# Gated linear attention groups: outputs ahead of the sample states' products, their sums behind the next weight's split

## The reference, cut to what matters

```python
o = einsum('bhts,bhsv->bhtv', att, vc) + einsum('bhtk,bhkv->bhtv', qc * exp(b), S)
S = exp(b_last)[..., 0, :, None] * S + einsum('bhsk,bhsv->bhkv', kc * exp(b_last - b), vc)
...
oa = merge(rmsnorm(oa, gn_a)) * silu(ga)      # and the same for GLA: ob
x = x + concatenate([oa, ob]) @ w_out
```

## Time and profile before

| what | us |
|---|---|
| median of 3 runs | 2837.17 |
| the profiled execution, its own time | 2839.51 |
| its span (first to last instruction) | 2837.9 |
| PE busy, share of the span | 2686.3, 95% |
| VectorE busy | 1864.8, 66% |
| ScalarE busy | 1282.3, 45% |
| GpSimd busy | 1343.1, 47% |

### The profile page before, as it was taken

How to read it: one execution, slowest core, us unless ns; L and a number is a source line. 1 busy time by engine, 2 the same in 40 slices (tenths; PEclk the granted TensorE clock), 3 DMA queues, 4 the chain that set the end, 5 groups by cost and what they waited for, 6 DMA issues and landing times.

```text
span 2837.9 us, 52238 instructions
## 1 busy us (share of the span) xinstructions
PE 2686.3 (95%) x19130; PEld 2546.6 (90%) x19130; DVE 1864.8 (66%) x2876; ACT 1282.3 (45%) x2311; POOL 1343.1 (47%) x1458
## 2 busy tenths in 40 slices
PE   7899999999989999998899999999998999999996
PEld 7899999888888999998899998787887789899996
DVE  7878866754547887758877864352635257877765
ACT  5565554222135566545565652222222225565552
POOL 3577743432225778613677753120303014777731
PEclk9999999999989999999999999999999999999998
DMA  3233322121112323232233223332333322223321
GB/s 128 72 95 98 92 93 77 62 74 54 46 60 69 96 88 97 86 105 68 67 104 94 87 99 141 112 119 87 118 113 121 104 85 76 86 87 105 92 95 54
DMA packets 109044, 255.71 MB, mean 90 GB/s; under 512 B 12496, under 2 KB 37216, under 8 KB 108800
## 3 DMA queue, kind: packets, MB, share of 16 engines
q1 hardware_dynamic: 96192, 206.73, 22.7%
q0 software_dynamic: 12608, 45.75, 4.4%
HBM read 227.65 MB, written 24.77 MB: 89 GB/s over the span
## 4 chain that ended last, share of the span: by engine, by line
PE 57%; DVE 7%; issue 3%; ACT 3%; POOL 1%; DVEq 0%; ACTq 0%; POOLq 0%
PE ps L981 27%; PE ps L568 12%; PE ps L590 11%; PE ps L837 1%; PE ps L901 1%; ACT wh L1108 1%; DVE ff_hidden_sums L1965 1%; PE ps L845 1%; ACT ps L1277 1%; DVE wl L1617 1%; PE ps L822 1%; DVE ff_x_low L1841 1%; DVE ff_blocks_b L1936 1%; DVE wl L1862 1%; PE ps L911 1%
## 5 line engine op out<-in xcount | busy, mean ns | idle before, releaser
L1862 DVE TENSOR_TENSOR wl<-ps,wh 128x512 fp32r<-128x512 f32 (+1 forms) x480 | 303.5, 632 | 150.7 <-ACT ps L1277 82.8
L1617 DVE TENSOR_TENSOR wl<-raw,wh 128x1024 fp32r<-128x1024 f32 x169 | 226.5, 1340 | 201.3 <-ACT wh L1108 200.6
L1108 ACT ACTIVATE wh<-raw 128x1024 fp32r<-128x1024 f32 x169 | 178.4, 1056 | 399.0 <-PE ps L568 200.8
L981 PE MATMUL ps<-ff_x_high,wh 128*128 128x288 f32 x1152 | 342.0, 297 | 12.6 <-DVE ff_c L1890 12.6
L981 PE MATMUL ps<-ff_x_low,wh 128*128 128x288 f32 x1152 | 341.3, 296 | 0.0
L981 PE MATMUL ps<-ff_x_high,wl 128*128 128x288 f32 x1152 | 340.4, 296 | 0.0
L590 PE MATMUL ps<-xh,wh 128*128 128x288 f32 x1248 | 299.4, 322 | 19.0 <-DVE xl L1639 15.2
L1277 ACT ACTIVATE ps<-ff_w_sums 128x512 f32<-128x512 f32 (+1 forms) x352 | 190.7, 551 | 269.0 <-POOL ff_w_sums L2550 261.6
L981 PE MATMUL ps<-ff_x_high,ff_more_high 128*128 128x288 f32 x864 | 256.2, 297 | 24.6 <-DVE ff_hidden L1899 10.3
L590 PE MATMUL ps<-xh,wl 128*128 128x288 f32 x1248 | 272.3, 300 | 0.0
L590 PE MATMUL ps<-xl,wh 128*128 128x288 f32 x1248 | 270.4, 299 | 0.0
(11 more groups left out here) (343 smaller groups left out, 7374.3 us busy)
## 6 DMA issues: line engine op xcount, KB each, us to landing
raw<-in_w SPq DMA_DIRECT2D x169, 512.0 KB, 3.5
raw<-in_w SPq DMA_DIRECT2D x288, 256.0 KB, 2.6
raw<-in_w SPq DMA_DIRECT2D x192, 192.0 KB, 2.3
rS<-in_s_ret POOLq DMA_DIRECT2D x28, 512.0 KB, 6.9
out_ret_s<-rS POOLq DMA_DIRECT2D x28, 512.0 KB, 3.7
x<-in_xT SPq DMA_DIRECT2D x8, 288.0 KB, 6.6
out_yT<-x SPq DMA_DIRECT2D x8, 288.0 KB, 2.2
S<-in_s_hgrn POOLq DMA_DIRECT2D x4, 512.0 KB, 3.6
```

The source lines that it names most:

```text
L981: last = nc.tensor.matmul(bank(w, q), lhsT=slot(w, q, wt)[:, t], rhs=rhs, start=(k == 0 and (wt, r) == (0, 0) and q in (1, 5, 2)), stop=(k ...
L1108: nc.scalar.activation(wh[:, n.mod(2), :], raw[:, r, :], ACT.Copy).then_inc(S("hi_made"), 1)
L1617: nc.vector.tensor_tensor(wl[:, n.mod(2), :], raw[:, n.mod(NRAW), :], wh[:, n.mod(2), :], ALU.subtract)\
L1862: nc.vector.tensor_tensor(slot(w, q, 1)[:, c], src[:, c], slot(w, q, 0)[:, c], ALU.subtract)\
```

## The change

In PE's table `state_sample` and `outputs(0)` change places. For HGRN it is now outputs behind quarter 1 of unit 3 and sample products behind quarter 2. For GLA the outputs of head 0 stand alone behind quarter 1 of unit 5, and the sample products behind the outputs of head 1. `outputs(0)` now waits itself for the last picks and for St, as `state_sample` did. VectorE's work on the sample states is in two functions: the decay product stays where it was, now followed by `keys_ready`; the sum goes behind the split. In the last group both go behind the second head's `heads_output`, and GpSimd does `heads_low` before the store of Sn and waits for the stores afterwards.

```diff
                     pe.wait_ge(S("S0_in"), count("S0_in", G("S0_in", 16)))
+                    pe.wait_ge(S("picked"), count("picked", G("picked", 8 * ns)))
+                    pe.wait_ge(S("turned_out"), count("turned_out", G("turned_out", 2 * ns + 3)))
...
-                    (3, 0): [state_prompt], (3, 1): [state_sample], (3, 2): [lambda: outputs(0)],
+                    (3, 0): [state_prompt], (3, 1): [lambda: outputs(0)], (3, 2): [state_sample],
...
-                    (5, 0): [state_prompt], (5, 1): [state_sample, lambda: outputs(0)],
-                    (5, 2): [lambda: head_norm(ns, i, pair, 0)], (5, 3): [lambda: outputs(1)],
+                    (5, 0): [state_prompt], (5, 1): [lambda: outputs(0)],
+                    (5, 2): [lambda: head_norm(ns, i, pair, 0)], (5, 3): [lambda: outputs(1), state_sample],
...
-            dve.wait_ge(S("S0_in"), count("S0_in", G("S0_in", 16)))
-            Tb = U[:, TP:T].rearrange("p (b t) -> p b t", t=LS)[:, :, LS - 1:LS].broadcast_to([P, NBAT, P])
-            nc.vector.tensor_tensor(Sn[:, :, :], S0[:, :, :], Tb, ALU.mult).then_inc(S("s_new"), 1)
-            dve.wait_ge(S("s_new"), count("s_new", G("s_new", 1)))
-            dve.wait_ge(S("turned"), count("turned", G("turned", k + 1)))
-            nc.vector.tensor_tensor(Sn[:, :, :].rearrange("p (a b) k -> p a (b k)", a=2),
-                                    Sn[:, :, :].rearrange("p (a b) k -> p a (b k)", a=2), ps[:, 6:8, :], ALU.add)\
-                .then_inc(S("turned_out"), 1)
+            if not following:
+                return
+            sample_decayed(ns, i, pair)
             if following == "hgrn":
                 keys_ready(i, 1)
+            split(n + (2 * ns + 3))
+            sample_added(ns, i, pair)
             if following:
-                split(n + (2 * ns + 3))
...
                     heads_output(2, None, 1, 1, heads=[r])
+                sample_decayed(2, None, 1)
+                sample_added(2, None, 1)
...
+            if pair == 1:
+                heads_low(2, None, 1, 1)
             reached = early(pool, count("turned_out", G("turned_out", 2 * ns + 4)))
...
-            pool.wait_ge(S("S_out"), count("S_out", G("S_out", 32 * (s + 1) // ns)))
+            if pair != 1:
+                pool.wait_ge(S("S_out"), count("S_out", G("S_out", 32 * (s + 1) // ns)))
...
-                heads_low(2, None, 1, 1)
+                pool.wait_ge(S("S_out"), count("S_out", group_count("S_out", 2, None, 1, 32)))
```

More of the change, by code:

```diff
@@ L1810, in gated_group, with sample_decayed, sample_added @@
                         .then_inc(S(f"taken{(u + (2 * ns + 1)).mod(2)}"), 1)
+        def sample_decayed(ns, i, pair):
+            G = lambda name, k: group_count(name, ns, i, pair, k)
+            U = gU[:, :] if ns == 1 else decay[:, pair, :]
+            k = 2 * ns + 3
+            dve.wait_ge(S("S0_in"), count("S0_in", G("S0_in", 16)))
+            Tb = U[:, TP:T].rearrange("p (b t) -> p b t", t=LS)[:, :, LS - 1:LS].broadcast_to([P, NBAT, P])
+            nc.vector.tensor_tensor(Sn[:, :, :], S0[:, :, :], Tb, ALU.mult).then_inc(S("s_new"), 1)
+            dve.wait_ge(S("s_new"), count("s_new", G("s_new", 1)))
+        def sample_added(ns, i, pair):
+            G = lambda name, k: group_count(name, ns, i, pair, k)
+            dve.wait_ge(S("turned"), count("turned", G("turned", 2 * ns + 4)))
+            nc.vector.tensor_tensor(Sn[:, :, :].rearrange("p (a b) k -> p a (b k)", a=2),
+                                    Sn[:, :, :].rearrange("p (a b) k -> p a (b k)", a=2), ps[:, 6:8, :], ALU.add)\
+                .then_inc(S("turned_out"), 1)
         def ffn(norm, n, u, j0, units):
```

## The result

The changed kernel takes **2850.53 us** (median of 5 executions, 2840.91 to 2856.5) against 2837.09 for the kernel before beside it (5 executions, 2834.51 to 2839.3): a ratio of 1.0039, interval 1.0025 to 1.0053. That is slower, above the forecast of 2840.8 and above the range's upper end of 2846.5.

| execution, us | mean granted clock |
|---|---|
| 2840.91 | 0.981 |
| 2840.95 (the profiled one, span 2839.3) | 0.981 |
| 2850.53 | 0.978 |
| 2852.41 | 0.976 |
| 2856.5 | 0.974 |

A forecast was written before the change was run, and what follows sets the result against it. TensorE, busy 95% of the span, was taken to bound the kernel, so only its waits count. Terms 3.23 + 0.9 - 0.5 = +3.6 us gave 2840.8 us; range 2834.5 to 2846.5.

The forecast's parts named there:

- Step 1: HGRN group ends: outputs ahead of sample products only pass on the wait for St; gain 0.
- Step 2: Three HGRN-to-HGRN starts: the sum behind the split delays scaled queries, sigmoid, root and scores; +3.23 us, bounds 0 and 3.9.
- Step 3: First GLA start: GpSimd's store of Sn waits for the sum, delaying loads and second scores; +0.9 us, bounds 0 and 1.5.
- The 0 in the HGRN groups: HGRN starts, GpSimd's queue: the sum ends within 0.3 us of when PE wants it; cost 0, bound 0.3 each.
- Step 4: Last group: moved products gain 0.9 us, the decay product delaying the low part costs 0.4; together -0.5, bounds -3.2 and +1.6.
- Rival (a): Group starts or outputs behind the St wait: idle PE brings more clock dips, 1.7 us each; 2844 to 2846 us, chance 0.22.

The follow-up runs named there:

- e5: The kernel before with only TensorE's new order in the four HGRN groups and the two new waits in `outputs`: 2839.92 us, ratio 1.0016.
- e10: The changed kernel with VectorE's sum moved behind the scaled queries at the three HGRN starts: 2845.89 us, ratio 1.0041.
- e12: e10 with S0's load waiting for the decay product and the store of Sn behind level 2 of the next group: 2843.1 us, ratio 1.0014.
- e4: The kernel before with only the last group's part of the change: 2838.21 us, ratio 1.0002.
- e3: The changed kernel with the last group's old order back on TensorE, VectorE and GpSimd: 2848.76 us, ratio 1.0041.
- e0: The changed kernel again with no edit, 12 executions: 2844.56 us, ratio 1.0030 to the kernel before.
- e8: The kernel before with only VectorE's sum moved behind the split, at the five places with a following group: 2847.31 us, ratio 1.0042.
- e1: The changed kernel with the sum moved back ahead of the split: 2842.64 us, ratio 1.0019.
- e13: The changed kernel with the HGRN sample products moved from behind quarter 2 to behind quarter 3: 2836.74 us, ratio 0.9999.
- e7: e4 with the last group's sample products moved behind the second head's head sums and block 6: 2834.82 us, ratio 0.9995.

## Why the prediction was wrong

**Step 1, outputs ahead, 0: wrong, and the main reason why the result left the range.** The reasoning on waits held; the wait for St passed to L724 (0.25 us), and ScalarE still waited for the unit. It missed what TensorE's clock does when the products, four matmuls in 3.78 us at half clock, follow a quarter behind the outputs: a dip of 5.1 us in place of 1.7. In the HGRN groups alone (e5) it cost +3.4 ± 1.7 us of clock and +1.2 ± 0.6 besides, which is not explained; at the end of the first GLA group it cost 1.7 more in every trace.

**Step 2, the sum in the chain, +3.23: right in mechanism, near in size.** The root's wait went from 0.28 to 1.37, 1.40 and 1.39; the first two stretches grew by 1.36 and 1.25, for 1.14 each. The third start was set at 0.95 from a stretch with a dip in it, which had hidden part of the chain; at full clock it waits as the others do.

**Step 3, GpSimd's queue: right in mechanism, the wait too small.** The wait before the second scores of the first GLA group was forecast at 0.9 (bounds 0 and 1.5) and came as 1.60. How much of it lasts isn't shown: the stretches around it grew by 0.59 and 0.18 only, the second with the gain of the earlier outputs in it. The 0 in the HGRN groups held for the changed kernel, whose trace has no wait of L633 there, and by the reason given: "PE, itself late by then". But that is true only as long as the root is later, and it hides a second chain of nearly the same length. e10 took the first away and the second came up at about the same price; e12 took both, and the cost was gone. As the two run side by side their prices don't add.

**Step 4, the last group, -0.5 (bounds -3.2 and +1.6): inside.** e4 measured -1.0 ± 0.7 and e3 against e0 -1.4 ± 0.8 at full clock (the profiled execution shows -0.22). The half clock moved as step 4 feared, from the outputs to the products. The sign by which it was to be known failed: the wait for the low part should have shrunk and grew, 5.58 to 6.30. From the head sums to the low part's start it was 9.30 us before (789.48 to 798.78) and after (791.01 to 800.31), but TensorE, with less of that stretch at half clock, reached its wait 4.75 us behind the head sums for 5.26, and the low part then took longer. VectorE's timeline and GpSimd's after the change:

```profile
799.43 1.22 DVE L1817 TENSOR_TENSOR Sn<-S,decay 128x1024 f32<-128x1024 f32 x1
```

```profile
800.31 1.60 POOL L2516 TENSOR_TENSOR hid_low<-sqsum,hid_high 128x576 fp32r<-128x576 f32 x1 [8.91 <-ACT hid_high L1436]
```

The low part began 0.08 us behind ScalarE's high part (L1436, to 800.23), as before the change, and so was not held back in its start; but it ran beside the last 0.34 us of the decay product and took 1.60 us for 1.40 in the earlier trace rows. So the decay product cost 0.20 and not 0.4. It is 1.60 or 1.61 in all twelve traces in which the decay product lies there and 1.40 in the four in which it doesn't (before, e3, e5, e8). The Trainium skill, page "SBUF — State Buffer", section "SBUF: two separate sides", has the one that comes second wait for the other's whole instruction. The trace agrees in direction: the low part ended 1.26 us behind the decay product, near its 1.40 alone. But no run put another operation in the decay product's place, so the port as the cause is argued, not shown.

**The sum and the rivals.** At full clock +3.6 was forecast and +5.1 ± 0.8 measured: so with that number the forecast would have been 2842 instead of 2841, inside the range. What broke the range is the clock. Rival (a) named it, priced a dip at 1.7 (right for the old order), gave it 0.22 and ended the range at 2846.5. Its cause, more dips from idle time at the group starts (or behind the St wait), explains only the smaller part: e1 took the idle at the starts away and still lost 5.6 ± 1.6, while dips behind waits at the starts came to some 2.7 us on average in the traces that have them (e8). It had no term for a dip that is three times as long. The loss also differs between executions by 20 us, so that the median of five, 2850.53, lies 6 above that of the other twelve, 2844.56, which is inside the range: that the five fell outside it is in part chance. That three times of the kernel before lay within 5 us was read as quiet of the kernel after; it was quiet of an order in which the dips are short.

Open: why the clock falls behind the outputs in one execution and not in the next, why the order alone costs 1.2 ± 0.6 at full clock, and how much of the loss the waits at the starts make.

## What to carry to other kernels

Ask of a moved step not only what waits for it but which chains start behind it, on every engine's queue; two that end together must both be freed before a microsecond is won (e10, e12). Look too for what other work could fill the wait: here the products themselves could (e13). When the throttle plays a part, read span times clock and span times (1 - clock) apart, over ten executions or more: the first finds the waits, the second here mostly the order of thin and dense work on TensorE. Keep thin matmuls in one piece and let dense ones follow them; a wait for another engine's chain (e7) is a good place for products that nobody needs soon.

## What the hardware showed unexpectedly

Behind the same 16 thin matmuls of the outputs (128x8, 1.95 us) the clock falls to 0.50 in about the same share of cases whatever follows (13 dips and 15, in 8 traces each). What follows decides how long it stays: some 3.4 us with dense weight units behind (1.7 lost at half clock, 15 of 15), 10 us in nine cases of 13 with the four products (64x512) a quarter behind (5.1 lost). And a mean clock lower by 0.001 goes with some 2.2 us in the time (2840.91 at 0.981 to 2856.5 at 0.974), which is most of the spread between executions of the changed kernel.

A store on GpSimd's queue that waits for another engine holds up all that stands behind it. In e10 GpSimd stood 13.18 us before the store of Sn; store and load then took 0.54 us each, with 0.43 between them, and only behind them came the first decays gL. VectorE, whose picks stand behind its next step of gU, waited 2.59 us for them, and through it TensorE's second scores 1.3 to 1.8 us at four starts, though neither transfer was what anybody waited for there. With the load ahead of the sum and the store behind level 2 (e12) that wait is gone.
